# A fourth weight buffer for the input projection, and both halves' high-part products ahead of both halves' low-part products

## What is computed

```
a = RMSNorm(h);  z = a @ W_in            # the input projection, the part that is changed
h += concat[HGRN2(z_A) | GatedDeltaNet(z_B) | ConformerConv(z_C) | MultiScalePool(z_D)] @ W_out
h += PEER(RMSNorm(h))                    # product-key experts: most of the time
h += sigmoid(RMSNorm(h) @ W_gate) * (p[i] @ W_ple)
```

## Time and profile before

| | us |
|---|---|
| median of 3 runs | 3916.31 |
| lowest, highest | 3914.47, 3918.94 |
| the profiled execution | 3943.08 |
| its span, first to last instruction | 3941.1 |

### The profile page before, as it was taken

One profiled execution on the slowest core, in us unless ns is written; L12 is line 12 of the kernel. 1 busy time (PEld: TensorE's weight loads), 2 busy tenths in 40 slices (PEclk: granted clock), 3 DMA queues, 4 the chain that ended last, 5 costly groups with the idle time before them and its releaser, 6 DMA issues.

```text
span 3941.1 us, 61029 instructions
## 1 busy us (share of the span) xinstructions
PE 3799.1 (96%) x23924; PEld 3471.7 (88%) x23924; DVE 2864.9 (73%) x4855; ACT 1619.9 (41%) x2437; POOL 2318.6 (59%) x1500
## 2 busy tenths in 40 slices
PE   6989999999999999999988999999999999999998
PEld 6888599999999999999487876999999999999993
DVE  6664368964888869888676652799468887788785
ACT  4553145553333344443346432555533333443333
POOL 1132069897788656666212410889877784688881
PEclk9989999999999999999999899999999999999999
DMA  7531146666999999999465021566679999999983
GB/s 172 102 34 49 44 171 218 215 220 203 321 336 336 321 357 390 386 388 343 130 130 82 15 76 50 191 209 224 214 243 334 312 333 337 352 379 372 363 320 109
DMA packets 426397, 924.22 MB, mean 235 GB/s; under 512 B 95232, under 2 KB 242944, under 8 KB 424448
## 3 DMA queue, kind: packets, MB, share of 16 engines
q1 hardware_dynamic: 274368, 552.91, 41.1%
q0 software_dynamic: 96448, 291.90, 23.0%
q10 hardware_dynamic: 55296, 75.52, 5.2%
HBM read 797.01 MB, written 123.15 MB: 233 GB/s over the span
## 4 chain that ended last, share of the span: by engine, by line
PE 74%; POOL 13%; DMA 4%; DVE 3%; issue 3%; ACT 3%; another core or an unknown queue 0%; SPq 0%; ACTq 0%; DVEq 0%; POOLq 0%
PE banks L1460 29%; PE banks L1534 11%; PE banks L1472 8%; POOL u_stage L2262 5%; POOL peer_gates L2246 5%; PE banks L1515 3%; PE banks L1373 3%; PE banks L1389 3%; PE banks L1571 2%; DMA w_parts<-w_fm 2%; PE banks L890 1%; PE banks L1209 1%; PE banks L885 1%; PE banks L1196 1%; PE banks L887 1%
## 5 line engine op out<-in xcount | busy, mean ns | idle before, releaser
L2246 POOL DMA_INDIRECT peer_gates<-peer_v,u_stage x512 | 712.1, 1391 | 366.1 <-DVE peer_gates L2950 135.8
L1534 PE MATMUL banks<-gated_parts,v_parts 128*128 128x320 f32 x6144 | 904.7, 309 | 9.7 <-DVE gated_parts L2982 7.8
L1534 PEld LDWEIGHTS banks<-gated_parts,v_parts 128*128 128x128 f32 x6144 | 901.1, 188 | 13.5 <-issue 13.4
L1460 PE MATMUL banks<-peer_x_parts,u_parts 128*128 128x448 f32 x3168 | 662.5, 366 | 1.0 <-DVE u_parts L2920 1.0
L1460 PEld LDWEIGHTS banks<-peer_x_parts,u_parts 128*128 128x128 f32 x3168 | 590.1, 188 | 46.3 <-DVE u_parts L2920 1.7
L2262 POOL DMA_INDIRECT u_stage<-dense_gelus,u_stage x256 | 396.4, 1548 | 105.3 <-issue 77.5
L1460 PE MATMUL banks<-peer_x_parts,low_s 128*128 128x448 f32 x1696 | 399.6, 367 | 2.4 <-issue 2.2
L2934 DVE SCALAR_TENSOR_TENSOR normed<-peer_gates,u_stage,normed 128x1024 f32<-128x1024 f32 x254 | 326.1, 1284 | 93.2 <-DMA peer_gates<-peer_v,u_stage 78.1
L2254 POOL DMA_INDIRECT u_stage<-gelus,u_stage x256 | 345.4, 1349 | 77.7 <-issue 77.7
L2950 DVE SCALAR_TENSOR_TENSOR peer_gates<-peer_gates,u_stage 128x1024 f32<-128x1024 f32 x254 | 325.2, 1280 | 88.8 <-DMA peer_gates<-peer_v,u_stage 67.2
L2003 ACT ACTIVATE u_stage<-banks 128x448 f32<-128x448 f32 x256 | 138.9, 542 | 607.7 <-PE banks L1460 491.4
(11 more groups left out here) (392 smaller groups left out, 7234.7 us busy)
## 6 DMA issues: line engine op xcount, KB each, us to landing
v_stage<-peer_v SPq DMA_DIRECT2D x256, 512.0 KB
u_stage<-peer_ut SPq DMA_DIRECT2D x244, 512.0 KB, 5.0
dense_gelus<-u_stage ACTq DMA_DIRECT2D x256, 224.0 KB
gates<-peer_gates SPq DMA_DIRECT2D x16, 2560.0 KB
u_stage<-gates SPq DMA_DIRECT2D x64, 640.0 KB
gated<-dense_gelus SPq DMA_DIRECT2D x256, 160.0 KB
x<-peer_ut SPq DMA_DIRECT2D x64, 512.0 KB, 5.2
u_raw<-peer_ut SPq DMA_DIRECT2D x64, 512.0 KB, 4.7
```

What stands on the lines that cost most here:

```text
L1460: ins = mm(PS[:, d % 2, 0:DW], u_part(n, a, k), XR[:, b, k, DENSE0:TOK], start=(k == 0 and m == 0), stop=(k == KT - 1 and m == 2))
L1534: ins = mm(vc[k][:, 0:PW3], VR[:, s, b, k * 128:(k + 1) * 128], HR[:, s, a, :], start=(j == 0 and m == 0), stop=(j == NKEYS - 1 and m == 2))
L2246: eng.indirect_dma_start(out=GU[:, t % 4, :], out_offset=None, in_=din["peer_v"].rearrange("l i j d -> (l i j) d"), in_offset=bass.Indirec ...
```

## The change

- A fourth raw buffer (WF3) and a fourth low buffer (W3L), both laid over the part of the mixers' output (MIXT) that is written later. Tiles 0 to 11 rotate over four, tiles 12 to 19 over three (`RAW_SLOT`). So the load of tiles 4 to 14 waits for tile j - 4, of 15 to 19 for j - 3, and that of tile 3 for nothing.
- A third high buffer in each stretch (`HIGH_AT`), so that `wf_high(j)` waits for tile j - 3. ACT's calls move up by one tile: `wf_high(2)` ahead of the loop, `wf_high(j + 3)` behind `take(j)`, `wf_high(12)` behind the `zt` results. POOL's calls move with them: 0 to 14 in the first loop (the token-major adds behind tile 7), 14 + u/2 in the loop over units.
- `feature_half` becomes `feature_begin` (L885 and L887's groups) and `feature_end` (L890's). `feature_tile` begins p, begins s, ends p, ends s. Within `feature_begin` the wait for `x_low` moves from ahead of the first group to ahead of the second; the first waits for `x_high` alone.
- In layer 0, ACT makes the low start of tile 0 (`wf_negated`) behind `x_high(0, 2)`, and its high part behind `x_high(0, 1)` and the last `rms`.

```diff
+    RAW_SLOT = [j % 4 if j < FM_FIRST + 2 else (j - FM_FIRST - 2) % 3 for j in range(NFM)]
+    RAW_SLOT_USER = [max([i for i in range(j) if RAW_SLOT[i] == RAW_SLOT[j]], default=None) for j in range(NFM)]
+    HIGH_AT = [HIGH_EL, HIGH_LA] + [(HIGH_GB, HIGH_EL, HIGH_GA)[(j - 2) % 3] for j in range(2, FM_FIRST + 2)]
+    HIGH_AT += [HIGH_WT[:, 0], HIGH_GA, HIGH_GB] + [(HIGH_WT[:, 0], HIGH_WT[:, 1], HIGH_GB)[j % 3] for j in range(5)]
...
+            if RAW_SLOT_USER[j] is not None:
+                sp.wait_ge(pe_done, at("fm", L, RAW_SLOT_USER[j]))
...
-                    sp.wait_ge(pe_done, at("fm", L, j - NWF))
                     load_wf(L, j)
...
         def feature_half(L, j, part):
 
-            high, low = wf_high_at(j), WFL[:, j % NWF, :]
+            feature_end(L, j, part, feature_begin(L, j, part))
+
+        def feature_begin(L, j, part):
+
+            high = HIGH_AT[j]
             if part == "p":
                 pe.wait_ge(act_done, at("wf_high", L, j))
             c0, c1 = (0, HALF) if part == "p" else (HALF, TOK)
-            for i in range(3) if part == "p" else range(NT):
-                pe.wait_ge(*made("x_low", L, i))
+            tiles = range(3) if part == "p" else range(NT)
+            for i in tiles:
+                pe.wait_ge(act_done, at("x_high", L, i))
             pe.wait_ge(*bank_free())
             b = fill("z", L, j, part)
             for k in range(KT):
                 mm(b[:, 0:c1 - c0], high[:, k * 128:(k + 1) * 128], XH[:, k, c0:c1], start=(k == 0), stop=False)
+            for i in tiles:
+                pe.wait_ge(*made("x_low", L, i))
             for k in range(KT):
                 mm(b[:, 0:c1 - c0], high[:, k * 128:(k + 1) * 128], XL[:, k, c0:c1], start=False, stop=False)
-            pe.wait_ge(d_wlow[j % NWF], 16 * wf_lows(L, j))
+            return b
+
+        def feature_end(L, j, part, b):
...
+            pe.wait_ge(d_wlow[RAW_SLOT[j]], 16 * wf_lows(L, j))
...
         def feature_tile(L, j):
 
-            feature_half(L, j, "p")
-            feature_half(L, j, "s")
+            banks = [feature_begin(L, j, part) for part in "ps"]
+            for part, b in zip("ps", banks):
+                feature_end(L, j, part, b)
...
-            if j >= 2:
-                act.wait_ge(pe_done, at("fm", L, j - 2))
+            if j >= 3:
+                act.wait_ge(pe_done, at("fm", L, j - 3))
+            elif j == 2 and L:
+                act.wait_ge(dve_done, at("ple_done", L - 1))
...
             x_high(L, SAMPLE)
+            wf_high(L, 2)
...
                 take(L, j)
-                wf_high(L, j + 2)
+                if j + 3 < FM_FIRST + 2:
+                    wf_high(L, j + 3)
...
+            wf_high(L, FM_FIRST + 2)
...
-            for j in range(0 if L == 0 else 2, FM_FIRST + 4):
+            for j in range(0 if L == 0 else 2, FM_FIRST + 5):
                 wf_low(L, j)
-                if j == 6:
+                if j == 7:
...
-                if u % 2 == 0 and FM_FIRST + 3 + u // 2 < NFM:
-                    wf_low(L, FM_FIRST + 3 + u // 2)
+                if u % 2 == 0 and FM_FIRST + 4 + u // 2 < NFM:
+                    wf_low(L, FM_FIRST + 4 + u // 2)
```

More of the change, by code:

```diff
@@ L313, in trunk @@
     VM = region(4, NB, 64)
+    place["at"] = 4 * TOK
+    WF3 = region(D)
     place["at"] = 0
@@ L545, in trunk @@
     gated, v_done = sem("gated"), sem("v_done")
-    d_wlow = [sem(f"wf{i}_low_added") for i in range(NWF)]
+    d_wlow = [sem(f"wf{i}_low_added") for i in range(4)]
     d_wtlow = sem("wt_low_added")
     def wf_lows(L, j):
-        return len(range(j % NWF, NFM, NWF)) * L + j // NWF + 1
+        return RAW_SLOT.count(RAW_SLOT[j]) * L + RAW_SLOT[:j + 1].count(RAW_SLOT[j])
     d_row = [sem(f"row_gathered{i}") for i in range(4)]
@@ L738, in _ @@
             for j in range(FM_FIRST + NWF, NFM):
[L739 to L740 removed]
+                load_wf(L, j)
             for c in range(6):
@@ L885, in feature_half @@
                 mm(b[:, 0:c1 - c0], high[:, k * 128:(k + 1) * 128], XH[:, k, c0:c1], start=(k == 0), stop=False)
+            for i in tiles:
+                pe.wait_ge(*made("x_low", L, i))
             for k in range(KT):
                 mm(b[:, 0:c1 - c0], high[:, k * 128:(k + 1) * 128], XL[:, k, c0:c1], start=False, stop=False)
-            pe.wait_ge(d_wlow[j % NWF], 16 * wf_lows(L, j))
+            return b
+        def feature_end(L, j, part, b):
+            low = wf_low_at(j)
+            c0, c1 = (0, HALF) if part == "p" else (HALF, TOK)
+            pe.wait_ge(d_wlow[RAW_SLOT[j]], 16 * wf_lows(L, j))
             for k in range(KT):
@@ L1683, in x_high, with wf_high, wf_negated @@
             act.did(A(XH[:, :, cols], XT[:, :, cols], ACT.Copy).then_inc(act_done, 1), "x_high", L, i)
-        def wf_high(L, j):
+        def wf_high(L, j, split=False):
             if j >= NFM:
                 return
-            if j >= 2:
-                act.wait_ge(pe_done, at("fm", L, j - 2))
-            act.wait_ge(sem(f"wf{j % NWF}_loaded"), at("wf", L, j))
-            act.did(A(wf_high_at(j), WF[:, j % NWF, :], ACT.Copy).then_inc(act_done, 1), "wf_high", L, j)
+            if j >= 3:
+                act.wait_ge(pe_done, at("fm", L, j - 3))
+            elif j == 2 and L:
+                act.wait_ge(dve_done, at("ple_done", L - 1))
+            act.wait_ge(sem(f"wf{RAW_SLOT[j]}_loaded"), at("wf", L, j))
+            act.did(A(HIGH_AT[j], wf_raw(j), ACT.Copy).then_inc(act_done, 1), "wf_high", L, j)
+            if not split:
+                wf_negated(L, j)
+        def wf_negated(L, j):
             act.wait_ge(act_done, at("wf_high", L, j))
-            act.did(A(WFL[:, j % NWF, :], wf_high_at(j).bitcast(F32), ACT.Copy, scale=-1.0).then_inc(act_done, 1), "wf_negated", L, j)
+            act.did(A(wf_low_at(j), HIGH_AT[j].bitcast(F32), ACT.Copy, scale=-1.0).then_inc(act_done, 1), "wf_negated", L, j)
         act.wait_ge(sem("const_loaded"), at("consts"))
@@ L1702, in _ @@
                 rms(0, 3)
-                wf_high(0, 0)
                 x_high(0, 1)
                 rms(0, SAMPLE)
+                wf_high(0, 0, split=True)
                 x_high(0, 2)
+                wf_negated(0, 0)
                 wf_high(0, 1)
@@ L1735, in _ @@
             take(L, FM_FIRST)
-            wf_high(L, FM_FIRST + 2)
+            wf_high(L, FM_FIRST + 3)
             act.wait_ge(dve_done, at("cyc", L))
@@ L1745, in _ @@
             take(L, FM_FIRST + 1)
-            wf_high(L, FM_FIRST + 3)
+            wf_high(L, FM_FIRST + 4)
             act.wait_ge(dve_done, at("hla", L))
@@ L1785, in _ @@
             take(L, FM_FIRST + 2)
-            wf_high(L, FM_FIRST + 4)
+            wf_high(L, FM_FIRST + 5)
             for p in range(HUNITS // 2):
@@ L1789, in _ @@
                     take(L, FM_FIRST + 3 + p)
-                    wf_high(L, FM_FIRST + 5 + p)
+                    wf_high(L, FM_FIRST + 6 + p)
                 if p < HUNITS // 2 - 1:
```

23 lines of the change are left out of this document (15 added, 8 removed).

## The result

The changed kernel takes 3900.41 us (median of 20 runs) beside 3925.18 us for the kernel before (20 runs): ratio 0.9926, 95% interval 0.9909 to 0.9944, so 22 to 36 us faster. The medians differ by 24.8 us. The forecast was a gain of 40.0 us and a time of 3876.3 us, with a range from 3863 to 3892: the sign was right, the time lies 8 us above the range. Of the 24.1 us between forecast and result, 8.9 are the base: the first three runs of the kernel before had a median of 3916.31 us, all 20 have 3925.18. The other 15.2 us are gain that did not come, and they are what has to be explained. One run of a kernel in the experiments took 5639 us at a granted clock of 0.61, where all others have 0.92 or more, and is left out of every figure.

What follows compares the result with a forecast made beforehand. PE's waits for the DMA making the low part, 74.9 us in 22 places, were the target. Gains of 17.8 us (layer 0) and 22.2 (layer 1), together 40.0, took 3916.31 us to 3876.3; range 3863 to 3892.

Steps and rivals of the forecast that it cites:

- Tiles 2 to 9: Tile 2 to the token-major product: eight tiles take 51.1 us, gaining 12.4 us in layer 0 and 15.4 in layer 1.
- The cover behind it: Behind the token-major product: ACT loses 2.7 us waiting for `hf`, covered by about 4 us spare; PE sets tile 11's end.
- The load of tile 13: Behind the pooling stores in SP's queue: late landing costs 1 us a layer, kept between 0 and 4.3.
- the upper of the two bounds: Tile 13's load lands only when the last pooling store has, at 129.3 us, costing 4.3 us.
- Tile 14: Its 3.15 us wait goes, but PE then waits for DVE's queries ahead of a score unit: gain 0.
- Tile 18: Its low add goes out ahead of the qkv stores, ending PE's 5.05 us wait: gain 5.5 and 5.9 us.
- the part on depth and order: Input projections: copies start one tile earlier, the low part is needed after 17.1 us instead of 8.5, raw load's distance unchanged.
- The start: First groups of each layer wait for `x_high` instead of `x_low`: gain 0.9 us in layer 0, 1.9 in layer 1.
- an end: Layer 0 start: a shorter wait keeps the clock up for the slow 1.74 us group, 1.6 us more, not taken.
- Only the order helps: Rival: added depth void, six long waits each shrink by 2.1 us; with the starts 15.6 us, 3900.7 us; chance 0.05.
- the half gain: Rival: DVE's convolution becomes the bound behind tile 9, so only 21.7 us is gained, 3894.6 us; chance 0.13.
- Wrong if the time saved shows again as PE's wait for ACT or DVE: Sign against the forecast: saved time reappearing as PE's waits ahead of units 0 and 1; no size given.

Runs made afterwards that it cites:

- the repeat of the changed kernel: The changed kernel run again, unedited, as partner of three edited kernels: 3901.56 us beside 3928.63 us for the kernel before, ratio 0.9934.

## Why the prediction was right and wrong

**Tiles 2 to 9: right.** 12.4 and 15.4 us were forecast, 12.5 and 15.5 came. There is no wait for a low part, and the granted clock is 1.00 throughout, where it was 0.95 and 0.92 before.

**The cover behind it: right.** DVE has no gap at the second gated block any more. `hf` is done at 115.7 us, and ACT loads its table for the logarithm at 115.28, so even the wait of about 1 us for `hf` was hidden. The stretch to units 0 and 1 kept its 50 us, as PE sets it.

**The load of tile 13: right within its bounds.** SP, and then ACT, in the changed kernel:

```profile
114.49 0.44 SPq L752 DMA_DIRECT2D pool_s<-mixers  x1
114.97 4.50 SPq L714 DMA_DIRECT2D mixers<-w_fm  x2
```

```profile
124.60 1.06 ACT L1722 ACTIVATE high_el<-mixers 128x1024 fp32r<-128x1024 f32 x1 [4.58 <-DMA mixers<-w_fm]
```

It landed 9.6 us after its issue (10.5 in layer 1), against the 3.6 of the earlier trace rows. The last store ahead of it took 8.6 us (10.2 in layer 1). The load came in 1.5 us behind that store (0.8 in layer 1), which is the upper of the two bounds. Tile 14's load, issued at 119.14 us, landed after 10.4 us, 4.9 us behind tile 13's. The rule of the Trainium skill that was weighed there (DMA: Bandwidth & Descriptors, queues, rings and completion order) is that descriptors are consumed in ring order. The order of these landings agrees. The same section says that a later descriptor may finish its write before an earlier one, so ring order by itself does not forbid overtaking. No run here tells whether data were written out of order. ACT waited 4.58 and 5.46 us. It cost nothing in layer 0 and 0.5 us in layer 1; in the repeat of the changed kernel waits of 5.10 and 6.11 us cost 0.2 and 1.2. So ACT's spare time was some 4.9 us, where the prediction had 4. One us a layer had been taken.

**Tile 14: right, with its reason.** Its stall went and unit 3 stayed 17.4 us behind units 0 and 1 (17.43 before, 17.47 after). The prediction named "ACT's exponentials, whose place is the same". The experiments bear that out and show what fixes the place: with one pair of copies, 2.1 us, taken from ahead of the first exponentials, unit 3 comes 2.0 us earlier (15.43 us). The idle time ahead of it was 3.4 us in both layers, where 4 to 5 had been named.

**Tile 18: the step that failed.** The forecast was a gain of 5.5 and 5.9 us. The wait of 5.05 us for the low part did go, the wait of DVE for PE fell from 5.50 and 5.93 us to 3.48 and 2.26, and the stretch became longer all the same: DVE's waits for ACT's exponentials, behind those of the first round, went from 0.20, 0.32, 1.11 and 1.64 us to 3.65, 2.09 and 4.16 in layer 0. The failure sits in one sentence of the part on depth and order: "The raw load keeps the distance that it had, since it and its reader both moved up by one tile." For tiles 4 to 14 the load moved: it waits for tile j - 4. For tiles 15 to 19 it did not, since they rotate over three buffers as before. Only its reader moved, to directly behind the results of tile j - 3, which is the very event that the load waits for. For tiles 17 to 19 each landing, 3.6 to 5.8 us there, became a wait of ACT with the exponentials behind it (tiles 15 and 16 were spared by ACT's other work). "It lands after 3.6 us, within one tile" would have held with a tile between them. The edit that gives the load a round back removes 8 us a layer, 16 in all: the gap between the forecast 40.0 and the 23.7 by the stretches is 16.3. With that edit and without its 2 us in the first round the stretch is 67.9 us, beside the 67.4 that were forecast, so the size put on tile 18 was sound and the wait for the load is what it left out.

**The start.** 1.7 of 1.9 us in layer 1; 0.4 of 0.9 in layer 0, where the late low start of tile 0 made PE wait 4.09 us. The clock was up again for the first group of the s half, 1.31 us where the earlier trace rows has 1.74, which had been named as an end.

**The rivals.** None of them was this one. "Only the order helps" gave 3900.7 us and 3900.41 were measured, which is luck: the base had moved by 8.9 us, and its condition, that the added depth is void, did not hold. By the gain "the half gain" came nearest (21.7 us, 24.8 measured), but for another reason: the convolution never became the bound. "Wrong if the time saved shows again as PE's wait for ACT or DVE" was said of units 0 and 1 only; it showed ahead of units 3, 5, 7 and 9. The order alone has 18.1 us by the stretches, where that rival's sum for it, without the starts, was 12.8; but the depth by itself gave 27.6 us in the first stretch.

What stays open: why landings of the same 512 KB load vary from 3.6 to 5.8 us in the stretch was not tried, nor a fourth raw buffer for tiles 15 to 19, which would take the load's wait away where the copies stand.

## What to carry to other kernels

When a pipeline is made deeper, list for every stage and every index what its step waits for and where its reader now stands; the depth must grow in each stage that the reader is moved past, or the reader meets the transfer that it used to find done. An engine that makes parts for later must not wait for them ahead of work that others need now: put such copies behind the urgent work of the round, once the depth allows it (here 30 us beyond the change itself, and nothing without the depth). And where the rows show slow work behind a stall of PE, count that work too.

## What was not expected of the hardware

A load of 512 KB behind the pooling stores in the same queue landed after 9.6 and 10.5 us, where the median in the kernel before was 3.6 us; the median over all raw loads of the changed kernel is 5.3. In layer 0 PE's waits of 3.07, 3.40 and 3.81 us ahead of the score units were each followed by 8 matmuls in 2.05 us, the wait of 1.29 us by the same 8 in 1.14 us. In layer 1 of the repeat a wait of 3.29 us was followed by the 8 in 1.14 us, and only the next group, of 288 columns, ran slow (2.29 us, where 1.23 is usual). With the four waits gone, the granted clock in the stretch went from 0.89 to 0.97, and 5.7 of the 15.8 us that the stretch became shorter are busy time of PE (64.39 to 58.66), not idle time.
